# Gate rows laid out by head and chunk, an earlier convolution, and a substitution in smaller portions, in a hybrid recurrent decoder step

## The chip, the cores and the metric

The kernel runs on one core of a Trainium2 chip. The metric is the device time of one launch in microseconds; lower is better.

## The reference

One layer of a decoder trunk for 1024 prompt tokens and for 8 sequences of 4 sampled tokens (1056 columns in all; `T` in the code, of which `NS` = 32 are the sampled ones). Three token mixers take their inputs from one projection; only the parts that the change touches are written out here.

```python
proj = jnp.einsum('btd,dc->btc', rmsnorm(x), p['w_in'])
# gates of mixer A (mLSTM): i_log, f_log; gates of mixer B (gated DeltaNet): beta, logg
i_log = ml_i + p['ml_i_bias'];  f_log = log_sigmoid(ml_f + p['ml_f_bias'])
beta = sigmoid(gd_b);  logg = -exp(A_log) * softplus(gd_a + dt_bias)
# mLSTM, chunk by chunk: b = cumsum(f_log); mt = max(b + m, max_s<=t(b_t - b_s + i_s)); m = mt[-1]
# DeltaNet: q, k, v go through a causal convolution over 4 tokens and silu first
conv = silu(sum(buf[:, j:j + t_len] * cw[j] for j in range(4)))
# and per chunk: A = I + strict_lower(beta * (k k^T) * decay); sol = A^-1 [beta v, beta exp(G) k]
...
x = x + (gated sum of the three branches) @ w_out
x = x + relu(rmsnorm(x) @ w_up)^2 @ w_down
```

The running maximum `m` is a scan over all 1024 prompt tokens of a head: m_t = max(m_(t-1) + f_t, i_t).

## The kernel before

All large products are done in three passes (high part by high part, low by high, high by low), 128 output rows by 1056 columns at a time. Such a piece of work is a tile: 3 column groups of 352 by 8 blocks of the inner dimension by 3 passes, 72 matmuls, all recorded on line 367. For each tile ACT makes the high part of the weights (`make_hi`, L342), POOL the low part (`make_lo`, L348), and SP loads the weights (`load_w`, L321), two tiles deep: the load of a tile waits for the low part of the tile two before it. The three groups of a tile go to two PSUM banks in turn, `(3 * tile + g) % 2`, and a group starts only when ACT has evacuated the group two before it (`bank_free`).

There is no scheduler. Each engine runs a program written out by hand, in order. The small work of the mixers is placed between tiles, or inside them by a `Filler`: each call `slot()` issues a share of a tile (a ninth is a piece, 8 matmuls), and its ACT side evacuates a group and makes the next high part either at once, when the slot has more than 4 pieces, or only at the next call of `slot()` (the list `late`).

The order at the start of the layer is:

- tiles 0 and 1 (tile 0 holds the gate rows);
- `rows` (L1236 on), with tiles 2 to 6 as filler: the gate computations on 4 partitions (a head each) by 1056 columns. SP reads the rows back from DRAM, DVE and ACT compute, ACT writes the rows to DRAM (`rowd`), and PE transposes five of them into columns per token (`tok`);
- `conv_program`, tiles 7 to 16, with c = tile - 7. Tiles 2 to 13 are the twelve convolution tiles. Their results are evacuated into five buffers `u_in`. In round c, DVE does the convolution of tile c + 1 (`conv`, L477 to L482), the silu product of tile c (`cs`), the normalisation of tile c - 1 (`qn`), and in rounds 2 to 5 `inverse_blocks` (L639); ACT does the sigmoid of tile c (three activations), square and root; PE does the norm sums (`nq`, L512, rounds 0 to 7) and k by k products (L631, rounds 1 to 4). All of it is placed behind the dense tile of the round or between its evacuations;
- the substitution on POOL (`inverse_steps`, L680 and L683): 31 steps of two operations each, which invert the 32 by 32 diagonal blocks. SP carries the blocks to DRAM (`ld`) and back (`b_a`) first (`inverse_loads` 1 and 2). POOL does 8 steps after the low part of a tile, in rounds 6 to 9. DVE turns the result (`b_tt`, L688), SP writes it to DRAM (`td`) and reads it back as `d_t` and `d_tt`;
- the DeltaNet loop, two tiles a chunk: it begins on PE with L1718 (needs `d_qk` and `d_v`), then L1749 (needs DVE's `vb`, which stands behind `cl`, an operation that needs `d_z`), then L1772 (needs `d_t`, `d_tt`, and POOL's mask of DVE's `lt`).

SP's queue between the rows and the loop is: the loads of tiles 4 to 10 with the sixteen reads of G (`b_e`) after tile 8; then for each normalised tile c its store and the load of tile c + 11; the last stores come inside `gdn`'s first call, behind the reads of `d_qk` and `d_bc` and before those of `d_v` and `d_z`. `stored_all` before `d_z` waits for the stores of all tiles up to 16.

Of the kernel before, what the change touches and what calls it, by code (L numbers as in the profile page):

```python
# [9 lines left out]
ALU = mybir.AluOpType  # L10
# [20 lines left out]
NCH = SEQ // CH  # L31
TG = 3
# [10 lines left out]
NBUF = 5  # L43
# [80 lines left out]
def build(nc, xT, w_proj, w_half, w_full, par, con, rowpar, segrow, m0, conv0, st_ml, st_mn, st_gd, st_hg,  # L124
          yT, p_C, p_n, p_m, p_S, p_conv, p_H, s_C, s_n, s_m, s_S, s_conv, s_H):
    proj = nc.dram_tensor("proj", (NPROJ, P, T), F32, kind="Internal").ap()
    rowd = nc.dram_tensor("rowd", (7, H, T), F32, kind="Internal").ap()
# [3 lines left out]
    with ExitStack() as ctx:  # L131
# [30 lines left out]
        with ExitStack() as a:  # L162
            r_in = arena(a, "r_in", [H, 4, T])
            r_a = arena(a, "r_a", [H, 3, T])
            r_m = arena(a, "r_m", [H, T])
            r_row = arena(a, "r_row", [H, 7, T])
            r_tokens = arena(a, "r_tok", [H, 4, T])
            r_mp = arena(a, "r_mp", [H, 2 * NCH])
            r_t8 = arena(a, "r_t8", [H, DEC_BATCH])
            r_mo = arena(a, "r_mo", [H, 1 + DEC_BATCH])  # L170
            r_par = arena(a, "r_par", [H, 5])
# [5 lines left out]
            r_tok = {TOK_W: r_tokens[:, 0, :], TOK_EWS: r_tokens[:, 1, :], TOK_BETA: r_tokens[:, 2, :], TOK_KD: r_tokens[:, 3, :],  # L177
# [227 lines left out]
        def silu_names(c):  # L405
            return f"s{c} t{c}"

        cv_dve = steps("cv_dve", " ".join([conv_names(0)] + [f"{conv_names(c + 1)} {silu_names(c)}" + (f" n{c - 1}" if c else "") for c in range(NORMED)]
                                          + [conv_names(9), silu_names(8), "n7", conv_names(10), silu_names(9), conv_names(11), silu_names(10), silu_names(11)]))
        cv_act = steps("cv_act", " ".join([f"e{c} l{c} s{c} " + (f"u{c - 1} v{c - 1} w{c - 1} r{c - 1} " if c else "") + f"q{c}" for c in range(NORMED)]  # L410
                                          + ["e8 l8 s8 u7 v7 w7 r7"] + [f"e{c} l{c} s{c}" for c in range(9, NCONV)]))
        cv_pool = steps("cv_pool", "z h0 h1 h2 h3 h4 " + " ".join(f"p{c} s{c}" for c in range(NBUF - 1)) + " " + " ".join((f"h{c + 1} " if c + 1 < NCONV else "") + f"p{c} s{c}" for c in range(NBUF - 1, NCONV)))
# [48 lines left out]
        def conv_post(kind, eng, op, c):  # L461
# [28 lines left out]
            if op == "cs":  # L490
                if c == 0:

                    rows_done(eng)
# [35 lines left out]
        def conv_program(kind, eng):  # L529
# [5 lines left out]
            if kind == "dve":  # L535
                post("conv", 0)
                for c in range(NORMED):
                    post("conv", c + 1)
                    post("cs", c)
                    if c:  # L540
                        post("qn", c - 1)
                    if c == 1:
                        inverse_decay(kind, eng)
                    if 2 <= c < 2 + H:
                        inverse_blocks(kind, eng, c - 2)
                post("conv", 9)
                post("cs", 8)
                post("qn", 7)
                post("conv", 10)
                post("cs", 9)  # L550
                post("conv", 11)
                post("cs", 10)
                post("cs", 11)
                inverse_turned(kind, eng)
            if kind == "pool":
                for c in range(NBUF - 1):
                    conv_tails(eng, c)
            for t in range(SEG_HG, GD0):
# [8 lines left out]
                if kind == "act":  # L567
                    make_hi(eng, Tile(t + 1))
                    post("sig", c if c < NORMED else 2 * c - 8)
# [5 lines left out]
                    else:  # L575
                        post("sig", 2 * c - 7)
# [4 lines left out]
                if kind == "pool":  # L581
# [3 lines left out]
                    if c + NBUF - 1 < NCONV:  # L585
                        conv_tails(eng, c + NBUF - 1)
# [55 lines left out]
        def inverse_loads(sp, part):  # L642

            if part == 0:
                sp.wait_ge(rw_out, 16)
                rows_done(sp)
                for a in range(NQ):
                    for h in range(H):
                        src = rowd[ROW_G, h, 0:SEQ].rearrange("(n b c) -> b n c", b=NQ, c=BLK)[a]
# [582 lines left out]
        rw_in, rw_out, rw_mo, seg_ld = sem("rw_in"), sem("rw_out"), sem("rw_mo"), sem("seg_ld")  # L1232
# [1587 lines left out]
```

## Time and profile before

| | |
|---|---|
| median of 3 runs | 2374.18 us (2370.18 to 2377.29) |
| the profiled execution | 2381.34 us, its span 2379.4 us |
| busy PE / PE weight load | 2227.1 us / 2163.8 us of the span |
| busy DVE / ACT / POOL | 920.6 / 811.7 / 650.4 us |
| mean granted TensorE clock | 0.965 of full speed |

The durations in the profile belong to the one execution of 2381.34 us. An engine's line gives its busy time; matmuls overlap a little, so a PE line with no idle time in brackets is a PE at work without a break.

### The profile page before, as it was taken

To read this page: it belongs to the slowest core of one execution; us is meant where nothing else is said; L and a number is where in the kernel's file an instruction comes from. 1 tells how busy PE (TensorE), PEld (TensorE's weight loads), DVE (VectorE), ACT (ScalarE), POOL (GpSimd) and SP (SyncE) were. 2 spreads that over 40 slices of the span, in tenths; PEclk is the share of its full clock that TensorE was granted. 3 is DMA by queue.
4 is the path that set the end of the run, shared out by engine and by line. 5 is a ranking of instruction groups with operands and counts; after the bars stand their busy time and mean duration, and the time that the engine had idled before them with its cause. 6 is when DMAs were issued, how large, how long until landed. Compare 5 with 4: busy or idle time off the path is not lost.

```text
span 2379.4 us, 36768 instructions
## 1 busy us (share of the span) xinstructions
PE 2227.1 (94%) x14031; PEld 2163.8 (91%) x14031; DVE 920.6 (39%) x1345; ACT 811.7 (34%) x1438; POOL 650.4 (27%) x467
## 2 busy tenths in 40 slices
PE   4999699999999899999999799987999999999996
PEld 3999699999799899889999699987999999999996
DVE  5857533232455465134442355324211211212215
ACT  4356333322254544133332133225133132232242
POOL 1223923222345353211112122211212212212221
PEclk9999899999899999899998899998999999999998
DMA  4122456442133322345641454310211111111112
GB/s 156 56 63 90 149 152 174 117 142 94 51 108 104 110 90 74 96 143 143 176 133 54 158 175 139 117 64 27 58 31 48 57 31 53 49 35 53 53 32 86
DMA packets 190708, 222.47 MB, mean 93 GB/s; under 512 B 39932, under 2 KB 144252, under 8 KB 190508
## 3 DMA queue, kind: packets, MB, share of 16 engines
q1 hardware_dynamic: 167548, 181.89, 26.4%
q10 hardware_dynamic: 23088, 39.59, 4.4%
q8 instruction: 49, 0.80, 0.1%
q14 instruction: 23, 0.19, 0.0%
HBM read 162.20 MB, written 59.24 MB: 93 GB/s over the span
## 4 chain that ended last, share of the span: by engine, by line
PE 79%; DVE 9%; POOL 3%; issue 3%; DMA 2%; ACT 2%; SPq 1%; DVEq 0%; ACTq 0%; POOLq 0%
PE D L367 68%; DVE g_dq L920 2%; DVE m_rd L1936 1%; POOL b_t L683 1%; POOL b_u L680 1%; PE M L819 1%; DVE xn_lo L2146 1%; DVE g_lg L1108 1%; POOL w_lo L348 1%; PE M L1718 1%; DMA proj<-stage 0%; PE M L1807 0%; PE M L2049 0%; PE M L512 0%; ACT g_sg L851 0%
## 5 line engine op out<-in xcount | busy, mean ns | idle before, releaser
L367 PE MATMUL D<-xn_hi,w_hi 128*128 128x352 f32 x2808 | 943.8, 336 | 61.8 <-DVE xn_lo L2146 22.7
L367 PE MATMUL D<-xn_hi,w_lo 128*128 128x352 f32 x2808 | 915.8, 326 | 0.0
L367 PE MATMUL D<-xn_lo,w_hi 128*128 128x352 f32 x2808 | 915.5, 326 | 0.0
L367 PEld LDWEIGHTS D<-xn_hi,w_hi 128*128 128x128 f32 x2808 | 538.9, 192 | 86.3 <-issue 37.7
L367 PEld LDWEIGHTS D<-xn_lo,w_hi 128*128 128x128 f32 x2808 | 540.4, 192 | 4.6 <-issue 3.8
L367 PEld LDWEIGHTS D<-xn_hi,w_lo 128*128 128x128 f32 x2808 | 538.6, 192 | 0.0
L348 POOL TENSOR_TENSOR w_lo<-w_raw,w_hi 128x1024 fp32r<-128x1024 f32 (+1 forms) x105 | 244.4, 2328 | 705.7 <-ACT w_hi L342 705.7
L348 POOL TENSOR_TENSOR w_lo<-e,w_hi 128x512 fp32r<-128x512 f32 (+1 forms) x96 | 163.9, 1707 | 608.1 <-ACT w_hi L342 608.1
L367 PE MATMUL D<-y_hi,w_hi 128*128 128x352 f32 x960 | 311.6, 325 | 19.2 <-DVE y_lo L2209 14.4
L367 PE MATMUL D<-y_lo,w_hi 128*128 128x352 f32 x960 | 311.6, 325 | 0.0
L367 PE MATMUL D<-y_hi,w_lo 128*128 128x352 f32 x960 | 311.0, 324 | 0.0
L367 PEld LDWEIGHTS D<-y_hi,w_hi 128*128 128x128 f32 x960 | 181.8, 189 | 20.6 <-DVE y_lo L2209 15.0
L2381 DVE TENSOR_TENSOR acc<-acc,D 128x352 f32<-128x352 f32 x192 | 100.0, 521 | 251.0 <-PE D L367 251.0
L367 PEld LDWEIGHTS D<-y_lo,w_hi 128*128 128x128 f32 x960 | 181.8, 189 | 0.0
L367 PEld LDWEIGHTS D<-y_hi,w_lo 128*128 128x128 f32 x960 | 181.6, 189 | 0.0
L342 ACT ACTIVATE w_hi<-e 128x512 fp32r<-128x512 f32 (+1 forms) x96 | 73.9, 770 | 302.6 <-PE D L367 295.7
L386 ACT ACTIVATE stage<-D 128x352 f32<-128x352 f32 x183 | 83.4, 457 | 261.3 <-PE D L367 250.1
L342 ACT ACTIVATE w_hi<-w_raw 128x1024 fp32r<-128x1024 f32 (+1 forms) x105 | 100.6, 959 | 183.4 <-PE D L367 145.7
L2376 DVE TENSOR_TENSOR y_lo<-e_b,y_hi 128x352 fp32r<-128x352 f32 x48 | 26.1, 544 | 168.6 <-ACT y_hi L2373 168.6
L2376 DVE TENSOR_TENSOR y_lo<-stage,y_hi 128x352 fp32r<-128x352 f32 x48 | 25.2, 525 | 154.6 <-ACT y_hi L2373 154.6
L480 DVE SCALAR_TENSOR_TENSOR u_x<-u_in,prm,u_x 128x1080 f32<-128x1080 f32 x36 | 60.8, 1689 | 1.3
L2369 ACT ACTIVATE e_a<-D 128x352 f32<-128x352 f32 x48 | 22.3, 464 | 104.0 <-PE D L367 104.0
(428 smaller groups left out, 2355.6 us busy)
## 6 DMA issues: line engine op xcount, KB each, us to landing
w_raw<-in_w_proj SPq DMA_DIRECT2D x73, 512.0 KB, 3.7
proj<-stage ACTq DMA_DIRECT2D x61, 528.0 KB, 2.9
e<-in_w_full SPq DMA_DIRECT2D x32, 512.0 KB, 3.6
e<-in_w_half SPq DMA_DIRECT2D x64, 256.0 KB, 2.6
stage<-proj SPq DMA_DIRECT2D x24, 528.0 KB, 3.6
d_bc<-rowd SPq DMA_DIRECT2D x32, 256.0 KB, 6.0
m_in<-proj SPq DMA_DIRECT2D x32, 256.0 KB, 4.0
proj<-u_o SPq DMA_DIRECT2D x12, 528.0 KB, 2.9
```

The costliest lines, as they stand in the source:

```text
L342: nc.scalar.activation(w_hi[t.slot][:, 0:kt, :], buf[:, 0:kt * P].rearrange("p (k m) -> p k m", m=P), ACT.Copy).then_inc(w_hi_made, 1)
L348: nc.gpsimd.tensor_tensor(w_lo[t.slot][:, 0:kt, :], raw(t)[0][:, 0:kt * P].rearrange("p (k m) -> p k m", m=P), w_hi[t.slot][:, 0:kt, :].bi ...
L367: last = nc.tensor.matmul(D[b][:, 0:GN], w[t.slot][:, k, :], x[:, k, cols], start=(k == 0 and n == 0), stop=(k == kt - 1 and n == 2))
L386: nc.scalar.activation(stage[:, t.slot, g * GN:(g + 1) * GN], D[t.bank(g)][:, 0:GN], ACT.Copy).then_inc(bank_free[t.bank(g)], 1)
L480: eng.scalar_tensor_tensor(x, conv_in(c)[:, j + 1:j + 1 + CONV_LEN], tap(j + 1), x, ALU.mult, ALU.add).then_inc(*cv_dve.step(f"{now}{c}"))
L680: pool.tensor_tensor(part, b_a[:, k + 1:BLK, k:k + 1].to_broadcast([P, n, k + 1]), b_t[:, k, 0:k + 1].unsqueeze(1).to_broadcast([P, n, k + ...
L683: pool.tensor_tensor(b_t[:, k + 1:BLK, 0:k + 1], b_t[:, k + 1:BLK, 0:k + 1], part, ALU.subtract).then_inc(*iv_pool.step(f"t{k}"))
L819: i = eng.matmul(M[banks[h % 2][q]][:, :], kt[0:NS, h * HD:(h + 1) * HD], vx[0:NS, at:at + 512], start=True, stop=True)
L920: eng.tensor_tensor(cb(g_dq, hf, j * HF), b[:, :, hf:2 * hf], b[:, :, hf - 1:hf].to_broadcast([P, C4 // (2 * hf), hf]), ALU.subtract).then ...
L1108: eng.copy_predicated(g_at[0:N, 0:C4].rearrange(blocks, c=2 * hf)[:, :, hf:2 * hf], cst[0:N, msk + j * HF:msk + (j + 1) * HF].bitcast(mybi ...
L2376: eng.tensor_tensor(y_lo[:, m, cols], v, y_hi[:, m, cols].bitcast(F32), ALU.subtract).then_inc(f_lo, 1)
L2381: eng.tensor_tensor(acc[:, m - FT, cols], acc[:, m - FT, cols], D[t.bank(g)][:, 0:GN], ALU.add).then_inc(bank_free[t.bank(g)], 1)
```

## The change

The gate rows are laid out on 36 partitions: 32 rows for head and chunk (`RP` = 4 * 8) of 128 columns, and 4 rows for the sampled tokens of each head. The maximum is scanned within each chunk from a value of -1e30 (`loc`); PE brings the chunk ends to one partition, DVE scans the eight ends of each head, PE brings the values before each chunk back as a column (`prev`), and one operation joins them. `rowd` has the layout of the rows. Gate reads are five DMAs instead of one, the exponentials are joined into fewer activations, PE does 5 transposes of 36 rows instead of 45, and ACT copies the columns out with six activations instead of two.

The rows take tiles 2 and 3 alone (`ROW_SLOTS` = 8, 2, 5 and 3 pieces), and `conv_program` runs from tile 4 to tile 16 with c = tile - 4. There are 4 buffers `u_in`. The convolution of tile c + 1 now needs the tile that PE has just ended. The last convolutions have the same round as the others. The rows lie in memory that neither convolution nor substitution uses. POOL does 5 steps of the substitution in each of rounds 6 to 12. On SP, the reads of G come after tile 5, `ld` and `b_a` follow on each other in round 4, and all twelve stores stand in the loop.

```diff
-NBUF = 5
+NBUF = 4
...
-            r_in = arena(a, "r_in", [H, 4, T])
-            r_a = arena(a, "r_a", [H, 3, T])
...
+            arena(a, "r_gap", [P, 13184])
+            r_in = arena(a, "r_in", [RP + H, 4, CH])
+            r_a = arena(a, "r_a", [RP + H, 3, CH])
...
             if kind == "dve":
                 post("conv", 0)
-                for c in range(NORMED):
-                    post("conv", c + 1)
+                for c in range(NCONV):
+                    if c + 1 < NCONV:
+                        post("conv", c + 1)
                     post("cs", c)
-                    if c:
+                    if 0 < c <= NORMED:
                         post("qn", c - 1)
...
                 if kind == "act":
                     make_hi(eng, Tile(t + 1))
-                    post("sig", c if c < NORMED else 2 * c - 8)
+                    if c < NCONV:
+                        post("sig", c)
                     evac_proj(eng, Tile(t), 0)
...
                     if c >= 6:
-                        inverse_steps(eng, range((c - 6) * 8, min((c - 5) * 8, BLK - 1)))
+                        inverse_steps(eng, range((c - 6) * 5, min((c - 5) * 5, BLK - 1)))
...
-                eng.dma_start(r_in[:, :, :], proj[ROWS_TILE, 0:4 * H, :].rearrange("(q h) t -> h q t", h=H)).then_inc(rw_in, 16)
+                eng.wait_ge(rw_zero, 2)
+                for q in range(4):
+                    eng.dma_start(r_in[0:RP, q, :], proj[ROWS_TILE, q * H:(q + 1) * H, 0:SEQ].rearrange("h (c n) -> h c n", n=CH)).then_inc(rw_in, 16)
+                eng.dma_start(r_in[RP:RP + H, :, 0:NS], proj[ROWS_TILE, 0:4 * H, SEQ:T].rearrange("(q h) t -> h q t", h=H)).then_inc(rw_in, 16)
...
-                eng.tensor_tensor_scan(r_m[:, 0:SEQ], r_in[:, 1, 0:SEQ], r_in[:, 0, 0:SEQ], 0.0, ALU.add,
-                                       ALU.max).then_inc(*rw_dve.step("m"))
-                for k in range(DEC_SEQ):
...
+                tt("fs", r_a[:, 1, :], r_in[:, 1, :], r_seg[:, 1, :], ALU.add)
+                scan("loc", r_l[:, :], r_a[:, 1, :], r_in[:, 0, :], MASKED, ALU.add, ALU.max)
+                slot()
+
+                eng.wait_ge(*rw_pe.after("ends"))
+                ts("cc", r_c[0:1, 0:2 * RP], M[1][0:1, 0:2 * RP], 0.0, None, ALU.add)
+                for h in range(H):
+                    at = slice(h * NCH, (h + 1) * NCH)
+                    scan(f"s{h}", r_c[0:1, 2 * RP:3 * RP][:, at], r_c[0:1, 0:RP][:, at], r_c[0:1, RP:2 * RP][:, at], 0.0, ALU.add, ALU.max)
...
+                eng.wait_ge(*rw_pe.after("prev"))
+                ts("pv", r_pv[:, 0:1], M[2][0:RP, 0:1], 0.0, None, ALU.add)
...
+                eng.scalar_tensor_tensor(r_m[0:RP], r_a[0:RP, 0, :], prev, r_l[0:RP], ALU.add, ALU.max).then_inc(*rw_dve.step("m"))
...
                 eng.wait_ge(*rw_dve.after("em"))
-                eng.activation(r_row[:, ROW_EM, :], r_row[:, ROW_EM, :], ACT.Exp).then_inc(*rw_act.step("em"))
-                eng.activation(r_row[:, ROW_ELW, :], r_row[:, ROW_ELW, :], ACT.Exp).then_inc(*rw_act.step("elw"))
+                eng.activation(r_row[:, ROW_ELW:ROW_EM + 1, :], r_row[:, ROW_ELW:ROW_EM + 1, :], ACT.Exp).then_inc(*rw_act.step("ex1"))
+                eng.activation(r_row[:, ROW_EG, :], r_row[:, ROW_G, :], ACT.Exp).then_inc(*rw_act.step("eg"))
                 eng.wait_ge(*rw_dve.after("kd2"))
...
+                eng.activation(r_tokens[:, 1:3, :], r_tokens[:, 1:3, :], ACT.Exp).then_inc(*rw_act.step("ex2"))
+                eng.wait_ge(*rw_dve.after("beg"))
+                eng.dma_start(rowd, r_row[:, :, :]).then_inc(rw_out, 16)
+                eng.dma_start(p_m.rearrange("h o -> o h"), r_mo[0:1, 0:H]).then_inc(rw_mo, 16)
+                eng.dma_start(s_m, r_mo[RP:RP + H, :]).then_inc(rw_mo, 16)
                 slot()
                 eng.wait_ge(*rw_pe.after("tok"))
...
             if kind == "pe":
-                for _ in range(5):
-                    slot()
-                eng.wait_ge(*rw_dve.after("mo2"))
-                eng.wait_ge(*rw_act.after("eg"))
+                slot()
+                eng.wait_ge(*rw_dve.after("loc"))
+                eng.transpose(M[1][0:1, 0:RP], r_a[0:RP, 0, last:CH], ident[0:RP, 0:RP])
+                eng.transpose(M[1][0:1, RP:2 * RP], r_l[0:RP, last:CH], ident[0:RP, 0:RP]).then_inc(*rw_pe.step("ends"))
+                slot()
+                eng.wait_ge(*rw_dve.after("mp"))
+                eng.transpose(M[2][0:RP, 0:1], r_c[0:1, 3 * RP:4 * RP], ident[0:1, 0:1]).then_inc(*rw_pe.step("prev"))
+                slot()
+                eng.wait_ge(*rw_dve.after("kd2"))
+                eng.wait_ge(*rw_act.after("ex2"))
                 for q in range(5):
...
-        SEG_ROW, SEG_HG = 2, 7
+        SEG_ROW, SEG_HG = 2, 4
...
-        ROW_SLOTS, ML_SLOTS = 6, 6
+        ROW_SLOTS, ML_SLOTS = [8, 2, 5, 3], 6
...
-            for t in range(4, 11):
+            for t in range(4, 8):
                 load_w(sp, Tile(t), w_proj[t])
-                if t == 8:
+                if t == 5:
                     inverse_loads(sp, 0)
-            for c in range(NORMED):
+            for c in range(NCONV):
                 conv_post("sp", sp, "store", c)
-                load_w(sp, Tile(c + 11), w_proj[c + 11])
+                if c + 8 <= LOOP_GD + 1:
+                    load_w(sp, Tile(c + 8), w_proj[c + 8])
                 if c == 4:
                     inverse_loads(sp, 1)
-                if c == 5:
                     inverse_loads(sp, 2)
```

## Rows read from the trace of the kernel before

**Rows 1.** The page, busy time of each engine over the span.

```profile
PE 2227.1 (94%) x14031; PEld 2163.8 (91%) x14031; DVE 920.6 (39%) x1345; ACT 811.7 (34%) x1438; POOL 650.4 (27%) x467
```

**Rows 2.** Waits of PE, 0 to 400 us: total, times, longest us.

```profile
PE D L367 <- POOL w_lo L348: 8.6, 2, 5.1
PE D L367 <- ACT u_in L441: 2.6, 1, 2.6
```

**Rows 3.** Chain that ended last, 0 to 500 us: start, us, what.

```profile
48.37 5.67 PE D L367 x24
...
201.65 1.78 PE M L631 x16
...
205.21 11.45 PE D L367 x72
...
333.46 1.78 PE M L1718 x16
...
368.91 1.78 PE M L1718 x16
```

**Rows 4.** Timeline of PE: start, us, what, and in brackets the idle time before.

```profile
116.82 0.65 PE L1368 MATMUL M<-cst,r_tok 4*128 4x4 f32 x8
...
294.33 3.79 PE L1718 MATMUL M<-d_qk 128*128 128x128 f32 x16 [13.40 <-DMA d_v<-proj]
...
304.28 1.15 PE L1772 MATMUL M<-d_t,d_mt 128*128 128x128 f32 x8 [0.47 <-DMA d_tt<-td]
```

**Rows 5.** Timeline of ACT and its DMA issues, 40 to 320 us.

```profile
65.51 0.47 ACT L386 ACTIVATE stage<-D 128x352 f32<-128x352 f32 x1 [3.35 <-PE D L367]
...
71.10 1.07 ACT L1330 ACTIVATE r_a<-r_a 4x1056 f32<-4x1056 f32 x1
...
109.25 3.77 ACTq L1350 DMA_DIRECT2D out_s_m<-r_mo  x1
...
281.75 0.34 ACTq L393 DMA_DIRECT2D proj<-stage  x1
```

**Rows 6.** Timeline of DVE, 40 to 320 us.

```profile
61.46 1.55 DVE L1260 TENSOR_SCALAR r_in<-r_in,r_par 4x1056 f32<-4x1056 f32 x2 [13.88 <-DMA r_in<-proj]
...
71.95 1.25 DVE L1264 TENSOR_TENSOR r_in<-r_m,r_a 4x1056 f32<-4x1056 f32 x1
...
80.38 2.32 DVE L1289 TENSOR_TENSOR_SCAN r_row<-r_tok,r_in 4x1056 f32<-4x1056 f32 x1
...
84.81 2.28 DVE L1264 TENSOR_TENSOR r_t<-r_in,r_mp 4x8 f32<-4x8 f32 x1
87.12 0.16 DVE L1264 TENSOR_TENSOR r_m<-r_t,r_in 4x8 f32<-4x8 f32 x1
...
201.48 6.12 DVE L480 SCALAR_TENSOR_TENSOR u_x<-u_in,prm,u_x 128x1080 f32<-128x1080 f32 x3
...
213.12 2.52 DVE L639 TENSOR_TENSOR b_l<-M,b_e 32x128 f32<-32x128 f32 x8
```

**Rows 7.** Timeline of POOL, 0 to 320 us.

```profile
232.55 0.25 POOL L680 TENSOR_TENSOR b_u<-b_a,b_t 128x31 f32<-128x31 f32 x1 [9.11 <-DMA b_a<-ld]
...
244.03 1.51 POOL L683 TENSOR_TENSOR b_t<-b_t,b_u 128x192 f32<-128x192 f32 x1
...
284.73 0.58 POOL L683 TENSOR_TENSOR b_t<-b_t,b_u 128x192 f32<-128x192 f32 x1
```

**Rows 8.** Timeline of SP's DMA issues, 0 to 330 us.

```profile
215.67 3.66 SPq L654 DMA_DIRECT2D ld<-b_l  x4
...
295.06 0.36 SPq L661 DMA_DIRECT2D td<-b_t  x1
```

**Rows 9.** Page of DMA issues, 0 to 330 us: KB each, median us to landing.

```profile
d_z<-proj SPq DMA_DIRECT2D x2, 256.0 KB, 6.7
```

**Rows 10.** POOL's groups, 230 to 295 us: busy us, mean ns.

```profile
L680 POOL TENSOR_TENSOR b_u<-b_a,b_t 128x31 f32<-128x31 f32 (+15 forms) x31 | 24.1, 777 | 11.2 <-DMA b_a<-ld 9.1
```

More of the change, by code:

```diff
@@ L31 @@
 NCH = SEQ // CH
+RP = H * NCH
 TG = 3
@@ L1229, in hgrn @@
                         slot()
-        rw_in, rw_out, rw_mo, seg_ld = sem("rw_in"), sem("rw_out"), sem("rw_mo"), sem("seg_ld")
-        rw_act = steps("rw_act", "e l ea be bl bs em elw ews kd eg tok toks")
-        rw_dve = steps("rw_dve", "i z az x ax bc mn fl mx sp g bcum gcum m "
-                       + " ".join(f"t{k} m{k}" for k in range(DEC_SEQ))
-                       + " mp0 mp1 mp2 u w lw1 lw2 em ew1 ew2 ng kd1 kd2 beg mo1 mo2")
-        rw_pe = steps("rw_pe", "tok")
+        rw_in, rw_out, rw_mo, rw_zero = sem("rw_in"), sem("rw_out"), sem("rw_mo"), sem("rw_zero")
@@ new lines, in build, with row_of @@
+        rw_act = steps("rw_act", "e l ea be bl bs ex1 eg ex2 tok toks")
+        rw_dve = steps("rw_dve", "i z az x ax bc mn fl mx sp g bcum gcum fs loc cc s0 s1 s2 s3 mz mp mo1 pv m sm1 sm2 u w lw1 lw2 em ew1 ew2 ng kd1 kd2 mo2 beg")
+        rw_pe = steps("rw_pe", "ends prev tok")
+        def row_of(q, chunk):
+            if chunk is None:
+                return rowd[RP:RP + H, q, 0:NS]
+            return rowd[0:RP].rearrange("(h c) q t -> c q h t", c=NCH)[bass.ds(chunk, 1), q].rearrange("x h t -> (x h) t")
@@ L1270, in mag, with scan @@
                     eng.wait_ge(*rw_dve.after(name))
+                def scan(name, out, a, b, first, o0, o1):
+                    eng.tensor_tensor_scan(out, a, b, first, o0, o1).then_inc(*rw_dve.step(name))
+                    eng.wait_ge(*rw_dve.after(name))
                 ts("i", r_in[:, 0, :], r_in[:, 0, :], r_par[:, 0:1], None, ALU.add)
@@ L1357, in rows @@
+                for q in range(5):
+                    i = eng.activation(tok[:, q, 0:NCH, :].rearrange("p c h -> p h c"), by_q[:, q, 0:RP].rearrange("p (h c) -> p h c", c=NCH), ACT.Copy)
+                i.then_inc(*rw_act.step("tok"))
+                eng.activation(tok[0:NS, :, NCH, :], by_q[0:NS, :, RP:RP + H], ACT.Copy).then_inc(*rw_act.step("toks"))
                 slot()
             if kind == "pool":
-                for _ in range(6):
+                for _ in range(4):
                     slot()
@@ L2560, in rest_of_conv @@
             def rest_of_conv():
-                for c in range(NORMED, NCONV):
-                    conv_post("sp", sp, "store", c)
                 sp.wait_ge(*cv_pool.all_of(1))
@@ L2745, in constants @@
     c[:, CC_BLK:CC_BLK + 32] = np.arange(32)[None, :] < s % 32
-    at = np.arange(T)
-    row = np.where(at < SEQ, at % CH != 0, (at - SEQ) % DEC_SEQ != 0)
-    return c, np.tile(row.astype(np.float32), (H, 1))
+    row = np.zeros((RP + H, 2, CH), np.float32)
+    row[:, 0] = 1
+    row[RP:, 0] = np.arange(CH) % DEC_SEQ != 0
+    row[RP:, 1] = np.where(np.arange(CH) % DEC_SEQ != 0, 0, MASKED)
+    return c, row
 def tiles(w, k_tiles):
```

141 lines of the change are left out of this document (58 added, 83 removed).

## The prediction

> **What bounds the kernel now.** I read the page first, then PE's waits, then the chain, then the timelines of each engine between 40 and 340 us. PE is busy 94% of the span [rows 1], and almost all of that is dense tiles, so time can only come from places where PE stands. The reader is to see four such places in the stretch that the change touches: 2.65 us in tile 2, where ACT evacuates late because it does the gate exponentials first (the 2.6 in [rows 2]); twice PE waits for the low part of the weights (8.6 us together, [rows 2]), because POOL does a portion of the substitution before it; and 13.40 us before the DeltaNet loop [rows 4]. Between them tile and small products follow without a gap: 11.45 us for a tile, 1.78 us for a block of k products [rows 3], the same for a norm sum. After an idle time PE is also slow: 24 matmuls right behind one took 5.67 us [rows 3], where 24 of the 72 in 11.45 us take 3.82, so each such stop costs 1.85 us more.
>
> From 333.46 us on chunks follow every 35.45 us (368.91 - 333.46, [rows 3]), with PE never idle. What the change is worth is how much earlier chunk 1 of the loop begins; nothing behind it gives that back, because PE sets the pace from there on.
>
> **The gate rows.** PE comes to tile 2 at 65.5 us (tile 1's last evacuation, [rows 5]). A piece is 11.45 / 9 = 1.27 us. Prices on 128 columns: two-input operations cost 1.25 us at 1056 columns and 0.16 at 8 [rows 6], so about 0.32 with the gap; a tensor_scalar 0.25 (from 0.78 at 1056, half of [rows 6]'s 1.55); a scan 0.45 (from 2.32); an activation 0.3 (from 1.07, [rows 5]) and 0.4 for two rows.
>
> First half, to `loc`: the inputs came at 61.46 [rows 6]; four more DMA issues of at most 0.5 us make it 63.5; six operations end by 65.3. ACT is free only at 66.4, behind the evacuation and store of tile 1, so the extra DMAs cost nothing. Two activations and nine DVE operations bring `loc` at 70.4. PE asks for it after 8 pieces, at 75.7: 5.3 us of cover, enough even if one small operation is held as the 4 by 8 one was at 84.81 (2.28 us against 0.16, [rows 6]). The exponentials now cover 2 us instead of 7, so the 2.65 us stop goes. The eight small operations to `mp` (0.2 each) end near 77.5; PE asks at 78.4. No cost.
>
> Second half: `prev` is there at 78.7. Fourteen operations to `kd2` take 3.7 us (82.4), the joined exponential 0.4, `beg` 0.3: 83.1. Then ACT issues three DMAs. Only behind them does it call its third slot, and the evacuation of tile 2's last group sits in `late` until that call, since the second slot has but 2 pieces. PE needs this bank for group 1 of tile 3, after 12 pieces: 65.5 + 15.3 + 0.3 for three small transposes = 81.1. So a new stop arises. The issues: 0.5 + 0.3 for the first two, and for the third between 0.3 (like tile 16's 0.34) and the 3.77 that it took [rows 5]. I take 1.3, near the low end, since the row transfer before it is now one run per partition. Evacuated at 85.7, PE idle 4.6 us. Then 6 pieces 7.64, 1.85 of slow clock, 0.5 for five transposes (45 took about 2.6: five times [rows 4]'s 0.65 for 8 less overlap): tile 3 ends at S = 95.7, bounds 94.7 and 98.2. The rows thus give nothing by themselves; they let ten tiles' worth of convolution start three tiles earlier.
>
> **The convolution.** Thirteen tiles, 8 norm sums and 4 products: 13 * 11.45 + 12 * 1.78 = 170.2 us. DVE may now start a convolution only when the tile before the present one is in. That is 3.1 us before the present tile starts in rounds 1 to 5 (k and norm products follow the dense part), 1.3 before in rounds 6 to 8, 0.5 after from round 9. In round 5 of before the three long operations began at 201.48, in front of tile 12 (205.21), and the blocks ended at 215.64 [rows 6], 10.4 after the tile's start; PE asks at 11.45. So rounds 3 and 4 have a margin of 1 us, and only round 2, behind the G decay of round 1 (four operations, 5.7 us), is late by some 0.75 us. Four buffers instead of five cost nothing: a buffer is refilled four tiles on, and its convolution ends within one. The reads of G and the loads behind them end near 104, tile 6 needs its weights at 109. SP's loads come a whole tile ahead; they had been earlier, which no one used.
>
> **The substitution.** Rounds start at S + 0, 13.2, 28.3, 44, 59, 74, 87, 100.5, 114, 125, 137, 148, 159.5. The last blocks are done at S + 84.5; `ld` takes 3.66 us to issue [rows 8] and about 4 to land, `b_a` about 5: POOL starts at S + 97.3, where before 16.9 us lay between (215.64 and 232.55, [rows 6, 7]), as a store stood in between. An operation of 192 columns takes 0.58 us free and 1.51 beside DVE [rows 7]; the mean was 0.78 [rows 10]. Free, five steps of the middle take 7.5 us, beside DVE up to 15; DVE is busy for 9 to 10.5 us of each round. POOL then does: round 7 from S + 105.7 to 115.5, low part to 118.7, round 8 to 131, low part to 134.2, round 9 to 147, low part to 149.3 where PE wants it at 148.1 (1.2 us late), round 10 to 157, low part 159.5, round 11 to 164, end at S + 168 to 169. So the substitution ends before tile 16, and of the two stops for weights (8.6 us) about 1.2 stays. Cover gone, each us that POOL needs more per round in rounds 8 to 10 is a us on PE.
>
> Tile 16 ends at S + 170.2 + 2.0 = 267.9, where before it ended at 280.9 (its last evacuation is over just before the store at 281.75, [rows 5]). Gain so far 13.0.
>
> **Into the loop.** Before, td was issued at 295.06 [rows 8] and L1772 ran at 304.28 [rows 4], 9.2 later. What is late next is `d_z`: SP asks first that tile 16 be stored (3.7 us after PE's end, 0.85 to the issue and 2.9 to land), and `td` is queued behind it: issued at +4.3, so L1772 at +13.5 from there. By the other branch `d_z` lands at +10.5 (6.7 us, [rows 9]); DVE's `cl`, which needs it, stands in front of `db`, `lt` and `vb`, and then come POOL's mask and L1749: L1772 at +14.2. I take the later: 282.1. Without that wait it would be +7.4, so PE loses about 7 us here. `d_v` is behind the store of tile 11 and the load of tile 18 and lands at S + 174.5, 2.3 us after tile 16; that hides under the same 14.2. From L1772 to chunk 1 29.2 us as before (333.46 - 304.28, which holds the slow clock of the stop): 311.3 against 333.46.
>
> **Sum.** 22.2 us. The profiled execution had 2381.3, so 2359.1 there; it was 7.2 above the median of 2374.2, and against this the same saving gives 2352.
>
> **A rule weighed.** In [rows 7] one operation takes 0.58 or 1.51 us, and [rows 6] shows a DVE operation of 0.16 taking 2.28 beside a POOL subtraction. The Trainium skill (SBUF — State Buffer, section "Who interferes with whom") says that a DVE instruction with two SBUF inputs and a GpSimd one that reads SBUF lock each other out for a whole instruction. The trace agrees. By that rule alone, with DVE never pausing, each step would pay the full turn; this is the first rival.
>
> **Rivals.**
> - POOL is held all the time: sixty operations of 1.6 us instead of 0.86 with the gap. Rounds 7 to 11 then need 16 + 3.2 us each against 11.45 to 13.2, PE waits some 34 us for low parts, tile 16 ends near 301 and L1772 at 315, 10.6 later than before: 2385. It turns into a loss from about 1.3 us an operation. Against it: the mean of 0.78 was measured with DVE just as full, and DVE is free from round 11. Chance 0.05.
> - POOL is held somewhat more than I count (1.05 us an operation): about 10 us more on PE, 2362. For it: conv, product and POOL now share every round. 0.17.
> - DVE becomes late each round: margin 1 us in rounds 2 to 4; two or three us over it cost 7 in all, 2359. 0.08.
> - The new stops are small: third issue 0.3 us, td and z quicker, POOL never late: gain 30, 2344. 0.15.
> - The change does not do what it says: a load or `d_v` comes so late that the loop starts as before, 2374. Against it: nothing on SP waits for anything later than tile 16's store. 0.04.
>
> **Numbers.** The likeliest case has 0.51: 2352, its own range 2346 to 2358 (the third issue -1 to +2.5, POOL -1 to +3, the way into the loop +-2). With the others 2341 to 2366. A change under 0.3% (7 us) can hardly be told from none: faster 0.88 (the four gaining cases, less 0.03 for what I do not see), same 0.05, slower 0.07.
>
> **What would show it.** `loc` near 70 us with PE at work; one stop of PE at 81 us, ended by ACT's L444 evacuation, 3.5 to 7 us; tile 4 near 96; tile 16's end near 268; substitution from 193 to 264; L1718 near 270 and L1772 near 282, released by DVE, POOL or `d_tt`; chunks every 35.45 us from 311. Wrong if PE waits for `w_lo` in rounds 8 to 11 by more than 5 us, if small products in rounds 1 to 8 wait for DVE, or if chunk 1 begins after 326.

## The result and the profile after

The changed kernel took 2359.9 us, the median of 7 executions (2350.9 to 2367.6), beside 2374.2 for the kernel before in the same series (7 executions, 2367.1 to 2381.1). The ratio is 0.9938, with a 95% interval of 0.9920 to 0.9957: 14.3 us saved, where 22.2 were forecast. Run once more on another chip (after_again, below) it came to 0.9934 (0.9912 to 0.9956). The profiled execution took 2363.8 us, its span 2362.0.

The page, busy time of each engine [rows 1]. PE has nearly the same work (2227.1 us before); what changed is how long it stands.

```profile
PE 2221.9 (94%) x13994; PEld 2159.9 (91%) x13994; DVE 904.5 (38%) x1346; ACT 803.1 (34%) x1440; POOL 663.0 (28%) x469
```

The waits of PE from 0 to 400 us, in total, times, and the longest [rows 2]:

```profile
...
PE M L1729 <- DMA d_v<-proj: 3.8, 1, 3.8
PE D L373 <- ACT stage L392: 3.7, 1, 3.7
PE D L373 <- POOL w_lo L354: 3.4, 2, 2.7
PE D L373 <- ACT u_in L452: 3.0, 1, 3.0
PE M L1783 <- DMA d_tt<-td: 1.9, 1, 1.9
...
```

The wait for the low parts went from 8.6 to 3.4 us. Before the loop, the wait for `d_v` went from 13.40 us to 3.8 and the one for `d_tt` from 0.47 [rows 4] to 1.9. The fourth row is about as long as before's 2.6 us stop, but it is the new stop behind the gate's DMA issues. The second row lies ahead of everything that the change touches: PE's timeline has it at 48.13 us, and the kernel before has the same stop at 48.37 (3.71 us).

The windows view puts the end of the stretch in one line. Its columns are busy us and count of PE, PEld, DVE, ACT and POOL, then the granted clock, the DMA share and GB/s, here from 240 to 340 us:

```profile
240.00:340.00 100.00, 91.53 (x585) 90.15 (x584) 26.26 (x42) 27.05 (x51) 41.74 (x45) 0.93 0.55 157
```

The same window of the kernel before:

```profile
240.00:340.00 100.00, 76.93 (x471) 74.57 (x470) 49.71 (x54) 33.99 (x53) 66.60 (x65) 0.88 0.51 152
```

Fewer stops also bring fewer stretches at the lower clock behind them.

The chain that ended last, from the view for 0 to 400 us [rows 3]:

```profile
84.17 6.70 PE D L373 x24
...
247.20 24.61 PE D L373 x144
...
272.32 4.74 DMA proj<-stage
278.06 4.58 DMA td<-b_tt
...
292.17 7.19 DMA d_bc<-rowd
301.79 2.69 PE D L373 x15
...
317.98 1.78 PE M L1729 x16
```

Chunk 1 starts at 317.98 where before it started at 333.46 [rows 3], 15.5 us earlier, and chunks follow every 35.45 us as before. In this pair the 15.5 us are the gain of the whole kernel, for the rest of the span is 2044.0 us (2362.0 - 317.98) beside 2045.9 (2379.4 - 333.46). That the two agree so well is in part luck: over all traces of this document the rest is 2031 to 2046 us (after_again 2031.2, before_again 2041.2). No trace shows the gain given back behind chunk 1, so the reader can stop at 318 us, and three places of it are to be read.

**Tile 3 and the start of the convolution.** ACT's timeline [rows 5], then DVE's [rows 6]:

```profile
83.28 0.27 ACTq L1356 DMA_DIRECT2D out_s_m<-r_mo  x1
83.59 0.44 ACT L451 ACTIVATE u_in<-D 128x320 f32<-128x320 f32 x1 [1.28 <-issue]
```

```profile
69.03 2.66 DVE L1273 TENSOR_TENSOR_SCAN r_row<-r_seg,r_in 36x128 f32<-36x128 f32 x1
...
72.05 0.42 DVE L1273 TENSOR_TENSOR_SCAN r_l<-r_a,r_in 36x128 f32<-36x128 f32 x1
...
82.09 0.28 DVE L1264 TENSOR_TENSOR r_row<-r_row 36x128 f32<-36x128 f32 x1
```

One of the small scans took 2.66 us, beside POOL's low part of 69.02 to 71.41 us (its neighbour of the same size takes 0.42), and the cover took it: `loc` is there at 72.5, PE asks at 75.7. The last gate operation ends at 82.4, and three DMA issues later ACT frees the bank for which PE had been waiting since 81.15.

**The low parts.** POOL's timeline [rows 7] from the start of the substitution:

```profile
189.79 0.69 POOL L675 TENSOR_TENSOR b_u<-b_a,b_t 128x31 f32<-128x31 f32 x1 [1.24 <-DMA b_a<-ld]
...
215.89 0.69 POOL L465 COPY u_pt<-u_in 128x3 f32<-128x3 f32 x1
216.52 1.21 POOL L466 COPY u_c<-u_in 128x24 f32<-128x24 f32 x1
...
222.80 1.60 POOL L678 TENSOR_TENSOR b_t<-b_t,b_u 128x247 f32<-128x247 f32 x1
...
230.40 2.38 POOL L354 TENSOR_TENSOR w_lo<-w_raw,w_hi 128x1024 fp32r<-128x1024 f32 x1
...
242.71 0.67 POOL L678 TENSOR_TENSOR b_t<-b_t,b_u 128x247 f32<-128x247 f32 x1
...
244.80 2.35 POOL L354 TENSOR_TENSOR w_lo<-w_raw,w_hi 128x1024 fp32r<-128x1024 f32 x1
```

The same operation on 247 columns takes 0.67 us while DVE is idle and 1.60 beside DVE. POOL's groups from 185 to 300 us [rows 10], busy us and mean ns:

```profile
L678 POOL TENSOR_TENSOR b_t<-b_t,b_u 128x31 f32<-128x31 f32 (+15 forms) x31 | 26.3, 847 | 2.4
L675 POOL TENSOR_TENSOR b_u<-b_a,b_t 128x31 f32<-128x31 f32 (+15 forms) x31 | 22.9, 737 | 3.1 <-DMA b_a<-ld 1.2
```

49.2 us for the 62 operations, where before had 48.3: spread over seven rounds, POOL pays hardly more for working beside DVE. The two copies are the tails of the convolution, which POOL makes between the low part and the next steps.

**The way into the loop.** SP's DMA issues [rows 8], then PE's timeline [rows 4]:

```profile
264.95 3.79 SPq L2553 DMA_DIRECT2D out_s_conv<-u_c  x1
268.84 0.38 SPq L1538 DMA_DIRECT2D d_v<-proj  x1
...
277.52 0.50 SPq L656 DMA_DIRECT2D td<-b_t  x1
```

```profile
275.61 3.78 PE L1729 MATMUL M<-d_qk 128*128 128x128 f32 x16 [3.81 <-DMA d_v<-proj]
...
287.78 2.01 PE L1783 MATMUL M<-d_t,d_mt 128*128 128x128 f32 x8 [1.92 <-DMA d_tt<-td]
```

The substitution was over at 265.4, but `td` was issued at 277.5, behind the wait for tile 16's store (issued at 272.32, landed at 277.06). And `d_v` was issued only behind the two outputs of the convolution state, `out_p_conv` at 263.84 and `out_s_conv`, whose issue alone took 3.79 us.

### The profile page after: what moved, and what is told of

Same layout as the page of the kernel before. It is cut to its first block, busy times and chain, and to the rows that moved or that the text cites. A ratio compares the mean times of both kernels' runs of the same rounds, so it can differ in the third digit from the quotient of the medians.

```text
span 2362.0 us, 36702 instructions
## 1 busy us (share of the span) xinstructions
PE 2221.9 (94%) x13994; PEld 2159.9 (91%) x13994; DVE 904.5 (38%) x1346; ACT 803.1 (34%) x1440; POOL 663.0 (28%) x469
## 4 chain that ended last, share of the span: by engine, by line
PE 77%; DVE 10%; issue 4%; POOL 4%; DMA 3%; ACT 2%; SPq 1%; DVEq 0%; ACTq 0%; POOLq 0%
PE D L373 67%; DVE g_dq L915 1%; DVE m_rd L1948 1%; POOL b_t L678 1%; DVE xn_lo L2158 1%; POOL w_lo L354 1%; PE M L814 1%; POOL b_u L675 1%; DVE u_x L487 1%; DVE g_lg L1103 1%; DMA proj<-stage 1%; PE M L1729 1%; ACT g_sg L846 1%; PE M L2092 0%; PE M L2061 0%
## 5 line engine op out<-in xcount | busy, mean ns | idle before, releaser
L373 PE MATMUL D<-xn_hi,w_hi 128*128 128x352 f32 x2808 | 945.4, 337 | 56.3 <-DVE xn_lo L2158 22.2
L354 POOL TENSOR_TENSOR w_lo<-w_raw,w_hi 128x1024 fp32r<-128x1024 f32 (+1 forms) x105 | 246.3, 2346 | 681.0 <-ACT w_hi L348 681.0
L373 PE MATMUL D<-y_hi,w_hi 128*128 128x352 f32 x960 | 311.7, 325 | 19.5 <-DVE y_lo L2221 14.3
L487 DVE SCALAR_TENSOR_TENSOR u_x<-u_in,prm,u_x 128x1080 f32<-128x1080 f32 x36 | 67.3, 1871 | 1.3
```

What stands on the lines that cost most here:

```text
L354: nc.gpsimd.tensor_tensor(w_lo[t.slot][:, 0:kt, :], raw(t)[0][:, 0:kt * P].rearrange("p (k m) -> p k m", m=P), w_hi[t.slot][:, 0:kt, :].bi ...
L373: last = nc.tensor.matmul(D[b][:, 0:GN], w[t.slot][:, k, :], x[:, k, cols], start=(k == 0 and n == 0), stop=(k == kt - 1 and n == 2))
L487: eng.scalar_tensor_tensor(x, conv_in(c)[:, j + 1:j + 1 + CONV_LEN], tap(j + 1), x, ALU.mult, ALU.add).then_inc(*cv_dve.step(f"{now}{c}"))
```

## The experiments

Twelve runs. "Chunk 1" is the start of the DeltaNet's second chunk on PE's timeline (333.30 in the profile of before, 317.82 in that of the changed kernel); it is read from one execution of each kernel, and executions of one kernel differ in it by about 1 to 2 us (before 333.30 and 333.99, changed 317.82 and 319.05, e1 below 325.86 to 327.60). Ratios are to the kernel before on the same chip.

### The rows alone: e1_rows, e1_again, e1_third

The kernel before with the new rows, spread over all of tiles 2 to 6; convolution and substitution as before.

```diff
-        ROW_SLOTS, ML_SLOTS = 6, 6
+        ROW_SLOTS, ML_SLOTS = [9, 9, 9, 18], 6
```

> The kernel before with the new layout of the gate rows alone: still tiles 2 to 6 beside the rows (portions of 9, 9, 9 and 18 pieces), convolution from tile 7 with five buffers, substitution 8 steps a round, SP's order as before. Theory A: in the kernel before tiles 2 to 6 took 66.4 us (65.5 to 131.95) for 57.3 us of matmuls, and the new rows take that away by themselves: tile 7 begins near 123, all behind it shifts by 8 to 9 us, the stops in front of w_lo (8.6 us) and d_v (13.4 us) stay; chunk 1 of the DeltaNet loop begins near 325, ratio to the kernel before 0.996. Theory B, as the prediction put it: the rows give nothing by themselves and only let the convolution start earlier; chunk 1 near 333, ratio 1.000.

> The rows alone once more, for a second trace. The first trace had chunk 1 at 326.0 and the rest in 2031 us, where the other traces have 2037 to 2046. Theory A: the rest of this kernel is as that of the others and the first trace was a lucky one: chunk 1 within 2 us of 326 again, the rest above 2037, so the gain of 7 us at chunk 1 is lost or hidden in how much of the run has the slow clock. Theory B: chunk 1 is later in most executions, above 329.

> The kernel before with the new layout of the gate rows alone, once more, for a mean over more executions. Theory A (the six microseconds that it brings chunk 1 forward are real, the spread of the executions hid them): ratio 0.997 to 0.999, chunk 1 at 326 to 328 us. Theory B (they are given back later): chunk 1 again at 326 to 328 us, ratio 1.000 or above.

Chunk 1 at 326.00, 327.60 and 325.86 us: 6 to 7.5 us earlier than before. Tile 7 starts at 124.5 us, not at 131.95: the 2.65 us stop is gone with the slow stretch behind it, and so is a second slow stretch, behind the 45 transposes. Those took 2.69 us (116.82 to 119.51; the five of e1_rows take 0.43), PE did not stand, and yet the granted clock over the next 4.9 us was 0.65. Theory A's positions came out, but theory B's ratio: 1.0001 (0.9983 to 1.0019) from 12 executions, and 0.9991 (0.9967 to 1.0015) from 12 more; the single execution of e1_again took 2373.2 us. The timeline of PE in e1_rows:

```profile
261.09 0.66 PE L373 MATMUL D<-xn_hi,w_hi 128*128 128x352 f32 x1 [7.51 <-POOL w_lo L354]
288.60 3.78 PE L1740 MATMUL M<-d_qk 128*128 128x128 f32 x16 [13.97 <-DMA d_v<-proj]
```

A stop of 2.89 us at 240.28 goes ahead of them. The large stops are all there, and from 240 to 340 us the granted clock is 0.88 as in before (0.93 in the changed kernel). So the rows alone are worth 0 to 2 us by the two ratios; the first interval excludes more than 4 us, the second reaches to 8. Whether the six microseconds at chunk 1 are lost behind it, and where, these runs don't settle.

### The substitution in four rounds: e2_sub8

```diff
-                        inverse_steps(eng, range((c - 6) * 5, min((c - 5) * 5, BLK - 1)))
+                        inverse_steps(eng, range([0, 8, 16, 24, 31, 31, 31, 31][c - 6], [0, 8, 16, 24, 31, 31, 31, 31][c - 5]))
```

> The changed kernel with 8 steps of the substitution in each of rounds 6 to 8 and 7 in round 9, instead of 5 in each of rounds 6 to 12. Theory A: PE comes to the weights of tiles 13 and 14 while POOL still has 16 operations to do in front of each low part; about 15 us of waits for w_lo instead of 3.4, in two places, so chunk 1 begins near 331 (317.98 in the changed kernel) and the time is that of the kernel before within 4 us. Theory B: POOL's work is the same in sum and ends earlier, so the way it is cut up does not matter: the time of the changed kernel, ratio to the kernel before 0.994.

Theory A. Ratio 0.9991 (0.9971 to 1.0011), chunk 1 at 329.31. The row of the waits of PE, 55 to 330 us, for the low parts:

```profile
PE D L373 <- POOL w_lo L354: 12.6, 3, 8.8
```

Eight steps a round stop PE for 8.8 us in tile 13 and for 1.9 before each of the next two low parts. With everything else of the change in place, 11.5 of the 15.5 us at chunk 1 are given back. The even spread is not a detail: without it the earlier convolution is worth nothing that the time shows.

### Spreading it by the width of the steps: e4_shape

```diff
-                        inverse_steps(eng, range((c - 6) * 5, min((c - 5) * 5, BLK - 1)))
+                        inverse_steps(eng, range([0, 7, 12, 16, 20, 23, 27, 31][c - 6], [0, 7, 12, 16, 20, 23, 27, 31][c - 5]))
```

> The changed kernel with 7, 5, 4, 4, 3, 4 and 4 steps of the substitution in rounds 6 to 12 instead of 5 in each: more where POOL had room, fewer in rounds 8 to 10. Theory A: the waits for w_lo of 0.77 and 2.65 us go, with the slow clock behind the second (1.7 us); tile 16 ends near 266.7 instead of 271.8, chunk 1 near 313, ratio to the kernel before 0.992. Theory B: the time goes to the way into the loop (d_v is behind the load of tile 18 and the sample's convolution state on SP), PE waits there about 5 us longer: chunk 1 within 2 us of 318.

The same row here:

```profile
PE D L373 <- POOL w_lo L354: 2.6, 2, 1.3
```

Two stops of 1.3 us each instead of 0.8 and 2.65, and neither has a slow stretch behind it. The chain has the two tiles behind the second stop:

```profile
248.35 23.18 PE D L373 x144
```

That is 0.3 us over two tiles at full clock (22.90), where the changed kernel has 24.61. Chunk 1 at 315.67, 2.2 earlier and between the two theories; ratio 0.9938 (0.9916 to 0.9959), that of the changed kernel. Only 0.3 of the 2.2 us stand at the end of tile 16 (271.54), for this execution was 0.9 us behind the other from the first stop on (85.03 for 84.17). The rest came after it: tile 16's store landed in 3.3 us, and L1783 started 14.6 us behind the tile's end instead of 16.0.

### One more piece before the first slot: e3_slot9

```diff
-        ROW_SLOTS, ML_SLOTS = [8, 2, 5, 3], 6
+        ROW_SLOTS, ML_SLOTS = [9, 2, 4, 3], 6
```

> The changed kernel with portions 9, 2, 4 and 3 of the two filler tiles instead of 8, 2, 5 and 3, so that tile 2 ends inside the first portion and its last group is evacuated there. Theory A: the stop of 3.02 us at 81 us and the slow clock behind it (24 matmuls in 6.70 us instead of 3.82) go, 5.9 us, and everything behind shifts: tile 4 begins near 89.5 instead of 95.2, chunk 1 near 312, ratio to the kernel before 0.9915. Theory B: it is given back later, because DVE then has less time between the end of the rows and the convolution of tile 4, or PE waits for the gate columns instead: chunk 1 within 2 us of 318.

The last group of tile 2 is now evacuated before the second half of the rows. What stops PE is the next bank, and less. Its timeline from 83 us:

```profile
87.20 0.43 PE L373 MATMUL D<-xn_hi,w_hi 128*128 128x352 f32 x1 [1.65 <-ACT u_in L448]
```

1.65 us at 87.20 and no slow clock behind it, against 3.02 and 2.9 in the changed kernel; chunk 1 at 313.07, 4.8 earlier, near theory A's 312. Ratio 0.9936 (0.9913 to 0.9959): on the time the 4.8 us can't be told from none.

This trace also shows something about the stop in front of tile 15, which is 2.57 us here and 2.65 in the changed kernel:

```profile
243.88 23.18 PE D L373 x144
```

Behind it the clock did not fall: 23.18 us, where the changed kernel has 24.61 for the same two tiles.

### Before the loop: e5_order, e7_z, e8_conv

e5_order issues `d_v` and `td` on SP ahead of the convolution's outputs and of the wait for tile 16's store:

```diff
                 prefetch(eng, None if sample else n, (gd_dve, "zs"))
                 if n is None and not sample:
+                    inverse_loads(eng, 3)
+                    slot(1)
                     stored_all(eng, GD0)
```

> The changed kernel with another order on SP at the way into the DeltaNet loop: d_v is read and the turned inverse (td) written before the two outputs of the convolution state and before the wait for tile 16's store, which d_z needs. Theory A: PE's 3.81 us wait for d_v goes, but L1760 and L1783 then wait for d_z's branch (DVE's clamp, mask of the gates, POOL's mask), 14 us behind the end of tile 16; chunk 1 begins 2 us earlier than in the changed kernel, near 316, and the ratio to the kernel before stays within the interval of the changed kernel (0.992 to 0.996). Theory B: d_v and td are what holds the loop up, and chunk 1 begins 5 to 6 us earlier, near 312, ratio 0.991.

`td` went out at 267.49 instead of 277.52, and the waits for `d_v` and `d_tt` were gone. In their place PE waited 5.77 us for `d_vb`, which needs `d_z`: theory A's wait, but without its 2 us of gain. Chunk 1 stayed at 318.02 (0.9927, 0.9901 to 0.9953). The chain that ended last, 268 to 320 us:

```profile
273.22 7.48 DMA proj<-stage
...
280.72 3.00 DMA d_z<-proj
...
286.25 2.08 PE M L1761 x8
```

The store of tile 16 now takes 7.48 us, not 4.74: `td`'s 1 MB and the outputs travel beside it. e7_z takes the store out of the way: the z rows of the first chunk are read from the place of the v rows, which was stored long before, so the z gate of that chunk is other data.

```diff
-                    stored_all(eng, GD0)
-                eng.dma_start(hn(B.z), pcols(GZ_TILE, 4, col0, N)).then_inc(gx_in if sample else gd_z, 16)
+                z_from = GD_TILE + 8 if n is None and not sample else GZ_TILE
+                eng.dma_start(hn(B.z), pcols(z_from, 4, col0, N)).then_inc(gx_in if sample else gd_z, 16)
```

> The queue order of e5_order, and the DeltaNet's z rows of chunk 0 read from the place of the v rows, which were stored long before, so that nothing that the start of the DeltaNet loads waits for the store of tile 16. What it leaves out: the z gate of the first chunk of the prompts is other data. Theory A (the branch behind tile 16's store, the transposes and then VectorE's gate and v*beta, holds L1783): L1783 starts at tile 16's end plus 7 to 9, near 279 to 281 us instead of 287.8, and chunk 1 near 309 to 311; ratio to the kernel before 0.988 to 0.990. Theory B (z isn't what holds it, the queue's order with TensorE's own work is): chunk 1 stays at 316 to 318 us, ratio 0.992 to 0.994.

The chain again, 255 to 300 us:

```profile
271.78 10.27 DMA d_z<-proj
282.08 0.06 DVE d_ze L1443
```

`d_z` is issued 5.3 us earlier than in the changed kernel and needs 10.27 us instead of about 3, and PE still waits 4.67 us for `d_vb`. The dependence is gone, the traffic took its place. Chunk 1 at 315.66: the issue of tile 16's store plus 43.0 us, where e5_order had 44.8 and the changed kernel 45.5. Ratio 0.9924 (0.9894 to 0.9955). These are nearly theory B's numbers, but not its mechanism, for PE waits for the z branch; what the chain shows is a third thing. e8_conv tests it with the right data: from e5_order, the convolution's outputs move behind the first `d_t` and `d_tt`.

```diff
                     inverse_loads(eng, 3)
-                    slot(1)
                     stored_all(eng, GD0)
...
+                if n is None:
+                    slot(1)
```

> e5_order with one more move: SyncE issues the two outputs of the convolution (162 KB in rows so short that they take 10 us to land) behind the DeltaNet's first d_t and d_tt, and not ahead of tile 16's store and the z rows; nothing else, and the output is complete. Theory A (the transfers of one another hold the DeltaNet's start: in e5_order tile 16's store took 7.5 us, in e7_z the z rows took 10.3 us, while td's stores and these outputs were under way): tile 16's store lands within 4 to 5.5 us of its issue, z is there 2 to 3.5 us earlier, chunk 1 starts 42 to 43.5 us behind the issue of tile 16's store instead of 44.8, near 315 us; ratio 0.990 to 0.992. Theory B (td's own 1 MB and tile 16's store are enough to fill the DMA engines, the outputs add nothing): 44.5 to 45 us behind it, ratio 0.992 to 0.994.

The chain of e8_conv, 268 to 320 us:

```profile
272.71 3.34 DMA proj<-stage
...
280.84 0.72 SPq L2555
...
290.25 6.31 DMA d_bc<-rowd
296.58 0.70 DVE d_de L1437
...
298.99 3.97 PE D L373 x15
```

Tile 16's store lands in 3.34 us instead of 7.48 and `d_z` at 279.0: the traffic of the outputs was the cause, theory A's own step. L1785 (the changed kernel's L1783) starts at 282.51, against 288.12 in e5_order. But of these 5.6 us 4.19 go again 16 us later, where PE waits for ACT, which waits for DVE's `d_de`, which waits for chunk 1's token rows `d_bc`, and the 15 matmuls behind this stop take 3.97 us instead of 2.4. The token rows' four reads were issued from 284.88 on, 3.0 us earlier than in e5_order, and yet landed at the same time (296.6): the issue took 6.33 us instead of 3.16, behind the outputs that now stand in front of them. Chunk 1 at 316.30, 43.6 us behind the store's issue, at the edge of what theory A gave; ratio 0.9939 (0.9918 to 0.9959), theory B's number.

### All three, and the changed kernel again: e6_all, after_again, before_again

e6_all joins the edits of e3_slot9, e4_shape and e5_order.

> The changed kernel with the three edits together: portions 9, 2, 4, 3 of the filler tiles, 7, 5, 4, 4, 3, 4, 4 steps of the substitution, and the order on SP of the run before. Theory A: the gains add, 4.7 + 2.1 + 2 us at chunk 1 (near 309 instead of 317.8) and some less slow clock: ratio to the kernel before 0.990, below the changed kernel's interval. Theory B: each takes away the same wait before the loop, and together they give what one gives: chunk 1 near 313, ratio 0.993.

> The changed kernel once more, for a second trace and for its time on the chip on which the others run. Theory A (the stops in front of the low parts and the later z rows are the kernel's own and not that execution's): stops of 3 to 4 us in sum before the low parts, L1783 16 us behind tile 16's end, chunk 1 at 317 to 319 us, ratio 0.993 to 0.995. Theory B (they were that execution's): chunk 1 at 311 to 315 us.

> The kernel before once more, for a second trace. Chunk 1 at 333 within 2 us, rest between 2031 and 2046; if chunk 1 lies 5 us earlier than in the first trace, the gains read at chunk 1 are overstated by that.

e6_all brings chunk 1 to 312.95, no earlier than e3_slot9 alone (313.07), which is theory B: it loses in front of the loop (6.6 us for `d_vb`, with tile 16's store landing in 8.3 us) what the low parts gave. Ratio 0.9924 (0.9895 to 0.9953). After_again: 0.9934; the stops before the low parts 3.6 us in sum, the waits for `d_v` 3.8 and `d_tt` 2.2, chunk 1 at 319.05, so the pattern is the kernel's and not that execution's. Before_again took 2377.1 us, with chunk 1 at 333.99 and stops of 2.71, 3.49, 6.32 and 13.14. None of the variants e3 to e8 is faster than the changed kernel by more than the intervals; all have 0.992 to 0.994. No run takes away the new order on SP or the earlier convolution by itself, so their shares of the gain aren't measured apart.

## Why the prediction was right, and by how much it was off

The forecast was 2352 us, range 2341 to 2366, faster with 0.88. The time was 2359.9. That lies outside the range that the likeliest case had for itself (2346 to 2358); the whole range holds it because the rivals had widened it. The mechanism held: the gain lies between the gate rows and chunk 1, and in the changed kernel's traces nothing behind it gives it back. Its size was 15.5 us at chunk 1 in place of 22.2. The missing 6.7 us, step by step:

- **Up to tile 4: right.** `loc` 72.5 for 70.4, PE stops at 81.15 for 81.1, tile 4 starts at 95.2 for 95.7. Two errors met: the third issue took 0.27 us and not 1.3, so the stop was 3.0 and not 4.6; but the 24 matmuls behind it took 6.70 us, 2.9 more than at full clock, and not 1.85 more. "The rows thus give nothing by themselves" was right for the changed kernel, and e1 measured 0 to 2 us, within its intervals, where they have more room.
- **The convolution: 1.2 us of low-part stops was 3.4, and the clock behind them was left out.** The start of the substitution came out early (189.8, forecast 193.0), its end at 265.4 (264), the k products wait 0.66 us (0.75). But round 8 ended at 230.4 for 226.7, and round 9's low part at 247.15 when PE wanted it at 244.55. The steps themselves are not what was mispriced: those of rounds 7, 8 and 9 took 10.7, 12.7 and 11.3 us for 9.8, 12.3 and 12.8. What has no term in the sum is POOL's copies of the convolution's tails (the two lines above: 1.8 us in front of round 8's steps, 2.6 in front of round 7's). They used up the early start, and from the low part to round 8's steps it was 5.2 us and not 3.2. Then the slow clock: 144 matmuls in 24.61 us instead of 22.90, 1.7 us. Tile 16 ended at 271.8 for 267.9: 3.9 of the 6.7. e4_shape shows that the length of POOL's portion sets the stop: with fewer wide steps in a round the largest is 1.3 us. That the slow stretch comes with the stop is not shown so simply, for e3_slot9 has a stop of 2.57 us at the same place and no slow stretch.
- **Tile 16 to L1783: 16.0 us for 14.2, by the other branch.** The prediction had 13.5 us by `td` and 14.2 by `d_z`, and took the later. `td`'s branch was the one that bound: PE waited 1.92 us for `d_tt`, while `d_vb`, which needs `d_z`, was ready at 282.64, before L1760 at 284.80 asked for it. Against its own 13.5 us `td`'s branch was 2.5 late: `td` was issued 5.7 us behind tile 16 and not 4.3, for the store was set down with 2.9 us to land and took 4.7, and L1783 came 10.3 behind that and not 9.2, for `td` took 4.6 us for 3.6. The prediction carried the landing times over from a place in which the outputs of the convolution state were not yet under way: before they were issued at 283.85 and 284.74, behind the store of 281.75. e5_order, e7_z and e8_conv show what they depend on: the same 528 KB took 3.3, 4.7 and 7.5 us (and 9.6 in e7_z), by what was under way beside them. `d_v`, which SP issued behind the same outputs, landed 3.8 us behind tile 16 and not 2.3; as forecast, this hid under the way by `td`.
- **L1783 to chunk 1: 30.2 us for 29.2.** The prediction took this stretch for PE's own work "which holds the slow clock of the stop". The first half was right, the second a misreading. The windows from L1772 (L1783) to the matmul that waits for chunk 1's token rows, before and after:

```profile
304.28:317.30 13.02, 12.37 (x89) 12.24 (x89) 2.67 (x7) 3.96 (x10) 4.07 (x2) 1.00 0.83 216
```

```profile
287.78:301.79 14.01, 13.93 (x88) 13.79 (x88) 1.79 (x4) 3.96 (x10) 4.09 (x2) 0.88 0.74 196
```

Before had no slow clock in it (granted 1.00) and 0.65 us of standing at its end. The changed kernel has the slow clock of the 1.92 us stop (0.88), 1.6 us, and stands for less than 0.1 us. In after_again the slow clock is missing and the stretch is 13.0 us again. The 0.65 us has a long way behind it. The chain of the kernel before, 290 to 334 us:

```profile
295.46 3.56 DMA td<-b_tt
...
308.41 6.46 DMA d_bc<-rowd
...
317.30 2.66 PE D L367 x15
```

From `td` on, the chain runs through SP's queue: the loads of `td`, and behind them, one after the other, chunk 1's weights, q and k, v and token rows. It is as long as PE's own work to within a microsecond, so that the waits view shows nearly nothing of it: PE stands at its end for 0.65 us before, less than 0.1 in the changed kernel, 0.62 in after_again, and 4.19 in e8_conv, where this way got longer. From the issue of `td` to that matmul it was 22.2 us before (317.30 - 295.06) and 24.3 after (301.79 - 277.52), and from there to chunk 1 16.2 in both. So `td` must come early, and with it SP's queue; how much that brings is capped by PE's own work behind L1783.

This is why each lever in front of the loop gave so little. There are two paths of nearly one length, `td` with SP's queue behind it and the z rows to `d_vb`, and their transfers slow each other. e5_order shortened the first and met the second; e7_z cut the second's dependence and met the traffic; e8_conv cleared the traffic of the second and put it on the first. That the three shortened different paths and ended within 2.4 us of each other (315.66, 316.30, 318.02) is shown; how short the way could be with both paths clear wasn't tried.

The rivals: "POOL is held all the time" and "no effect" didn't happen. "POOL is held somewhat more" (2362) gave nearly the time that was measured, but not by its mechanism: an operation took 0.79 us on average and 0.07 of gap, not 1.05. That its number fits is chance. e2_sub8 shows how near it lay: eight steps a round are enough to lose the gain. "DVE late" didn't occur in rounds 3 to 8.

The Trainium skill (DMA: Bandwidth & Descriptors, section "Queues, rings and completion order") says that SP's and ACT's queues are rings on the same 16 DMA engines, each of which takes turns between the rings that it has work for. The runs agree: ACT's store took 3.34 us with the outputs of SP's queue out of the way and 7.48 with them beside it.

## What to carry to other kernels

When work is moved forward in time, don't carry over the landing times of the stretch that it comes from: price a store by what travels beside it. And list everything that the engine does in the round into which the work moves, the small copies too: here 1.8 and 2.6 us of them in front of two rounds' steps were left out. A wait of 0.5 us can be the visible end of a chain that is as long as the path of the busy engine, so before a large wait is removed, the chain behind the next small one is to be followed back; here it ran through the order of issue of one DMA queue. And give each stop of 2 us or more a range for the slow clock, from nothing to the 1.5 to 3 us that stops of this length had here.

## What the runs showed of the hardware

- The slow stretch behind a stop isn't in proportion to it, and not the same for the same stop. A stop of 3.02 us cost 2.9 us more (24 matmuls in 6.70 us), one of 2.65 us 1.7 more, one of 1.30 us 0.3, and one of 1.65 us left the matmuls behind it at 0.43 and 0.32 us, the full-speed durations. But in front of tile 15 a stop of 2.57 us (e3_slot9) cost 0.3 and not 1.7, and behind one of 2.70 us (e7_z) the granted clock was 1.00.
- The clock can fall without a stop: behind the 45 small transposes of the kernel before, 2.69 us in which PE was busy all the time, it was 0.65 over 4.9 us.
- The same kind of DMA issue on ACT's queue, the write of `out_s_m`, took 0.27 us here, with a row transfer of one run per partition ahead of it, and 3.77 in the kernel before [rows 5]. Whether the row transfer's shape or the write's own (its source was 4 partitions in both) made it, no run tells.
- Executions of one kernel differ by 17 to 26 us, and it goes with the mean granted clock: from 2350.6 us at 0.975 to 2367.6 at 0.967 over 19 executions of the changed kernel, from 2359.2 at 0.973 to 2385.3 at 0.964 over 56 of the kernel before. An edit of 2 to 5 us can be read at chunk 1, but not on the time.
